# Down products' last tiles block by block, x split block by block, and table loads taken out

## The reference: two blocks of two layers each, one after the other

```
x = x + gate * (w_out(mixer(modulate(rms_norm(x)))))
u, g = split(conv3(modulate(rms_norm(x)) @ ffn_up))       # per token neighbourhood
x = x + gate' * ((silu(u) * g) @ ffn_down)                # "down": 2816 -> 1024
```

## Time and profile before

| | |
|---|---|
| median of 3 runs | 1775.49 us |
| profiled execution | 1770.85 us |
| its span | 1769.6 us |
| PE matmuls busy | 1638.8 us, 93% of the span |
| DVE / ACT / POOL busy | 963.8 / 647.9 / 467.9 us |
| granted TensorE clock, mean | 0.976 |

### The profile page before, as it was taken

One profiled execution on the slowest core, in us unless ns is written; L12 is line 12 of the kernel. 1 busy time (PEld: TensorE's weight loads), 2 busy tenths in 40 slices (PEclk: granted clock), 3 DMA queues, 4 the chain that ended last, 5 costly groups with the idle time before them and its releaser, 6 DMA issues.

```text
span 1769.6 us, 24218 instructions
## 1 busy us (share of the span) xinstructions
PE 1638.8 (93%) x9336; PEld 1314.4 (74%) x9336; DVE 963.8 (54%) x1906; ACT 647.9 (37%) x1229; POOL 467.9 (26%) x384
## 2 busy tenths in 40 slices
PE   7999999889999989989899899879999999999888
PEld 5555555358888878846567899878899998878777
DVE  4488888542222277557664788554555444233821
ACT  2442333043333332233333555443444444134511
POOL 1012201015555500022320111015555555013401
PEclk9999999999999999999999999999999999999999
DMA  9334323313222255424432455443444344325131
GB/s 350 113 119 143 103 101 120 131 71 107 96 95 96 95 169 196 159 65 156 148 126 96 155 185 182 155 148 120 132 140 145 134 133 130 125 85 182 60 125 36
DMA packets 63825, 231.16 MB, mean 131 GB/s; under 512 B 7408, under 2 KB 8432, under 8 KB 63456
## 3 DMA queue, kind: packets, MB, share of 16 engines
q1 hardware_dynamic: 60800, 218.65, 36.8%
q0 software_dynamic: 2192, 6.29, 1.1%
q10 hardware_dynamic: 720, 4.68, 0.7%
HBM read 228.55 MB, written 1.05 MB: 130 GB/s over the span
## 4 chain that ended last, share of the span: by engine, by line
PE 84%; DVE 9%; ACT 3%; issue 2%; DMA 1%; POOL 1%; SPq 0%; DVEq 0%; ACTq 0%; POOLq 0%
PE ps L232 17%; PE ps L250 10%; PE ps L251 10%; PE ps L252 10%; PE ps L1193 4%; PE ps L1194 4%; PE ps L1195 4%; PE ps L1623 3%; PE ps L724 3%; PE ps L240 3%; PE ps L714 2%; PE ps L617 2%; PE ps L294 1%; PE ps L1440 1%; PE ps L379 1%
## 5 line engine op out<-in xcount | busy, mean ns | idle before, releaser
L259 ACT ACTIVATE weights_rounded<-ring 128x1024 fp32r<-128x1024 f32 x196 | 205.0, 1053 | 108.2 <-PE ps L1195 108.2
L250 PE MATMUL ps<-h_hi,weights_rounded 128*128 128x512 f32 (+1 forms) x656 | 222.0, 338 | 5.0 <-POOL weights_rest L271 2.9
L251 PE MATMUL ps<-h_lo,weights_rounded 128*128 128x512 f32 (+1 forms) x656 | 221.6, 338 | 0.0
L252 PE MATMUL ps<-h_hi,weights_rest 128*128 128x512 f32 (+1 forms) x656 | 221.5, 338 | 0.0
L265 DVE TENSOR_TENSOR weights_rest<-ring,weights_rounded 128x1024 fp32r<-128x1024 f32 x128 | 175.3, 1371 | 76.2 <-ACT weights_rounded L259 76.1
L271 POOL TENSOR_TENSOR weights_rest<-ring,weights_rounded 128x1024 fp32r<-128x1024 f32 x68 | 163.4, 2405 | 162.7 <-ACT weights_rounded L259 162.7
L232 PE MATMUL ps<-h,ring 128*128 128x512 f32 (+1 forms) x496 | 197.9, 556 | 7.1 <-DVE h L470 7.1
L232 PEld LDWEIGHTS ps<-h,ring 128*128 128x128 f32 x496 | 95.6, 195 | 100.6 <-issue 92.6
L1164 DVE SCALAR_TENSOR_TENSOR scratch<-ps,vectors,scratch 128x510 f32<-128x510 f32 (+1 forms) x88 | 54.1, 615 | 194.6 <-ACT scratch L1124 194.4
L250 PEld LDWEIGHTS ps<-h_hi,weights_rounded 128*128 128x128 f32 x656 | 125.6, 191 | 18.7 <-POOL weights_rest L271 3.3
L1124 ACT ACTIVATE scratch<-ps,vectors 128x512 f32<-128x512 f32 (+1 forms) x88 | 59.1, 672 | 209.6 <-PE ps L252 199.1
(11 more groups left out here) (281 smaller groups left out, 3400.6 us busy)
## 6 DMA issues: line engine op xcount, KB each, us to landing
ring<-in_up SPq DMA_DIRECT2D x88, 512.0 KB, 3.5
ring<-in_ada_rest SPq DMA_DIRECT2D x80, 512.0 KB, 3.5
ring<-in_a_in SPq DMA_DIRECT2D x80, 512.0 KB, 3.5
ring<-in_down SPq DMA_DIRECT2D x44, 512.0 KB, 3.5
ring<-in_even SPq DMA_DIRECT2D x20, 512.0 KB, 3.7
ring<-in_ada_first SPq DMA_DIRECT2D x16, 512.0 KB, 8.7
ring<-in_wout SPq DMA_DIRECT2D x16, 512.0 KB, 3.5
ring<-in_odd SPq DMA_DIRECT2D x16, 512.0 KB, 4.8
```

What stands on the lines that cost most here:

```text
L250: te.matmul(bank[:, 0:n], wh[:, k, :], hi(k), start=k == 0, stop=False)
L251: te.matmul(bank[:, 0:n], wh[:, k, :], lo(k), start=False, stop=False)
L252: ins = te.matmul(bank[:, 0:n], wl[:, k, :], hi(k), start=False, stop=k == KD - 1)
L259: sc.activation(pair[0], place(*key), ACT.Copy).then_inc(*mark("rounded", *key))
```

## The change

1. `act_rsqrt` loads its table only in its first call, `(0, 0)`.
2. Down, both layers: tiles 0 to 18 as before. For tiles 19, 20 and 21 the block e becomes the outer loop: PE waits for 19 and 20, issues both for e = 0, 1, 2, waits for 21, and then goes e by e. Each bank signals when it is complete, and DVE's residual of block e waits for that bank alone. In layer 0 the mean's matmul of block e-3 is issued behind block e, and the last three at the end.
3. Layer 1: ACT rounds a0, a1, a2 within the down loop, behind the hidden blocks of j = 18, 19, 20; POOL forms their rests as soon as they are rounded, no longer behind the last residual. a1 and a2 lie in other places (`PAIR_A[4]` and `PAIR_FIRST`, in scratch), a0 and `PAIR_A[4]` move by 128 columns.
4. x is split block by block: ACT rounds block k behind residual k, DVE forms x_lo of block k-2 behind residual k. ACT's table load follows the last block.
5. Mixer a, first head: the first three products go through x together, block by block, into banks 0, 1, 2 (`pe_first_a`). Products 3, 4 and 5 follow as before, with two rotary turns behind 3 and 4 each. DVE waits for the mask behind the rotary work instead of ahead of it.

```diff
 def act_rsqrt(m, n):
-        sc.preload_act_table_set("natural_log_exp_and_others")
+        if m == (0, 0):
+            sc.preload_act_table_set("natural_log_exp_and_others")
...
 def pe_down(layer):
+        for j in range(FB - 3):
+            ready(j)
+            for e in range(KD):
+                block(j, e)
+        for j in (FB - 3, FB - 2):
+            ready(j)
+        for e in range(3):
+            block(FB - 3, e)
+            block(FB - 2, e)
+        ready(FB - 1)
+        for e in range(KD):
+            if e >= 3:
+                block(FB - 3, e)
+                block(FB - 2, e)
+            block(FB - 1, e)
+            if layer == 0 and e >= 3:
+                pe_down_mean(e - 3)
...
 def act_down(layer):
+            if layer and FB - 4 <= j < FB - 1:
+                act_round(("a", 0, j - FB + 4), a_pair(0, j - FB + 4)[0:1], a_free(0, j - FB + 4))
...
+        else:
+            for k in range(KD):
+                sc.wait_ge(*at("residual", "down", 1, k))
+                sc.activation(xhi(k), xk(k), ACT.Copy).then_inc(*mark("x_rounded", 0, k))
...
 def dve_down(layer):
-        ve.wait_ge(*at("product", "down", layer, FB - 1))
         for e in range(KD):
+            ve.wait_ge(*at("product", *down_bank(layer, e)))
...
+            if layer and e >= 2:
+                x_rest(e - 2)
...
+    def a_pair(i, s):
+        if i == 0 and s in (1, 2):
+            return (PAIR_A[4], PAIR_FIRST)[s - 1]
+        return PAIR_A[s % 5]
...
+        if i == 0 and s < 5:
+            return [[at("hidden", 1, FB - 1)], [], [at("hidden", 1, FB - 1)], [at("product", "down", 1, FB - 2)],
+                    [at("product", "a", 0, 1)]][s]
...
+    def pe_first_a():
+        for n in range(A_FIRST):
+            te.wait_ge(*at("rest_pool", "a", 0, n))
+        for k in range(KD):
+            te.wait_ge(*at("x_rest", 0, k))
+            for n in range(A_FIRST):
...
+                te.matmul(bank, wh, xhi(k), start=k == 0, stop=False)
+                te.matmul(bank, wh, xlo(k), start=False, stop=False)
+                ins = te.matmul(bank, wl, xhi(k), start=False, stop=k == KD - 1)
...
 def pe_mixer_a(i):
+            for x in ((2 * n - 6, 2 * n - 5) if i == 0 and n < 5 else (n - 1,) if n else ()):
...
 def act_mixer_a(i):
         if i == 0:
-            sc.wait_ge(*at("residual", "down", 1, KD - 1))
             sc.preload_act_table_set("exp_and_others")
-            round_tile(0, 0)
-            act_split_x(0, lambda k: at("residual", "down", 1, k))
-            round_tile(0, 1)
-            round_tile(0, 2)
...
 def pool_mixer_a(i):
         if i == 0:
+            for s in range(A_FIRST):
+                rest(0, s)
             po.wait_ge(*at("residual", "down", 1, KD - 1))
             po.dma_start(MASKA, d["masks"][:, MK_A:MK_A + 1152]).then_inc(*mark("mask_in", 2, step=16))
-            for s in range(3):
-                rest(0, s)
```

More of the change, by code:

```diff
@@ L1180, in pool_up, with down_bank, block, ready @@
                                  YS[4 * (fb % 2) + 2][:, 0:n], ALU.mult).then_inc(*mark("hidden", layer, fb))
+    def down_bank(layer, e):
+        return ("down", layer, FB - 1) if e == KD - 1 else ("down_bank", layer, e)
     def pe_down(layer):
         n = TOK if layer == 0 else SEQ
-        for j in range(FB):
+        def block(j, e):
             wh, wl = (v3(x, 128) for x in pair(j % PAIRS))
             hi, lo = (x[:, 0:n] for x in HID_T[j % 4])
-            if j == 0:
-                te.wait_ge(*at("convolved", layer, 2 * FB - 1))
+            b = BANK[e][:, 0:n]
+            te.matmul(b, wh[:, e, :], hi, start=j == 0, stop=False)
+            te.matmul(b, wh[:, e, :], lo, start=False, stop=False)
+            ins = te.matmul(b, wl[:, e, :], hi, start=False, stop=j == FB - 1)
+            if e == KD - 1:
+                ins.then_inc(*mark("product", "down", layer, j))
+            elif j == FB - 1:
+                ins.then_inc(*mark("product", *down_bank(layer, e)))
+        def ready(j):
@@ L1189, in pe_down @@
             te.wait_ge(*at("rest", "down", layer, j))
             te.wait_ge(*at("hidden_rest", layer, j))
+        te.wait_ge(*at("convolved", layer, 2 * FB - 1))
+        for j in range(FB - 3):
+            ready(j)
             for e in range(KD):
[L1192 to L1195, removed]
@@ L1196, in pe_down @@
-            ins.then_inc(*mark("product", "down", layer, j))
-        if layer == 0:
[L1198 to L1201, removed]
+                block(j, e)
[4 more added lines that the diff above has]
+            block(FB - 2, e)
@@ new lines, in pe_down, with pe_down_mean @@
+        ready(FB - 1)
[6 more added lines that the diff above has]
+                pe_down_mean(e - 3)
+        if layer == 0:
+            for e in range(KD - 3, KD):
+                pe_down_mean(e)
+    def pe_down_mean(e):
+        te.wait_ge(*at("x_squared", "down", e))
+        ins = te.matmul(BANK[0][:, 0:TOK], mean_d, sq_d[e % 2][:, 0:TOK], start=e == 0, stop=e == KD - 1)
+        ins.then_inc(*(mark("mean_part", e) if e < KD - 1 else mark("mean", (1, 0))))
@@ L1233, in dve_down, with x_rest @@
             dve_ada_bias(38, FB)
-        ve.wait_ge(*at("product", "down", layer, FB - 1))
+        def x_rest(k):
+            ve.wait_ge(*at("x_rounded", 0, k))
+            ve.tensor_tensor(xlo(k), xk(k), xhi(k).bitcast(F32), ALU.subtract).then_inc(*mark("x_rest", 0, k))
         for e in range(KD):
+            ve.wait_ge(*at("product", *down_bank(layer, e)))
             for s in ((0, 1) if layer == 0 else (1,)):
@@ L1241, in dve_down @@
             ins.then_inc(*mark("residual", "down", layer, e))
+            if layer and e >= 2:
+                x_rest(e - 2)
+        if layer:
+            x_rest(KD - 2)
+            x_rest(KD - 1)
     K1, V1 = BIG[:, 0:512], BIG[:, 512:1024]
@@ L1395, in build @@
     PTA = [BIG[:, 3456 + 512 * j:3968 + 512 * j] for j in range(4)]
-    PAIR_A = [(rounded("a_rounded_0", "big", 5504, D), rounded("a_rest_0", "big", 6528, D)), pair(0), pair(1), pair(2),
-              (rounded("a_rounded_4", "big", 7552, D), rounded("a_rest_4", "big", 8576, D))]
+    PAIR_A = [(rounded("a_rounded_0", "big", 5632, D), rounded("a_rest_0", "big", 6656, D)), pair(0), pair(1), pair(2),
+              (rounded("a_rounded_4", "big", 7680, D), rounded("a_rest_4", "big", 8704, D))]
+    PAIR_FIRST = (rounded("a_rounded_first", "scratch", 1024, D), rounded("a_rest_first", "scratch", 2048, D))
+    A_FIRST = 3
     TBA = [7, 6, 2, 5]
@@ L1446, in a_rope, with a_bank @@
         return ("a", i, x), BANK[4 + (x + 1) % 2]
+    def a_bank(i, n):
+        return BANK[n if i == 0 and n < A_FIRST else 6 + n % 2]
+    def pe_first_a():
[4 more added lines that the diff above has]
+            for n in range(A_FIRST):
+                wh, wl = (v3(w, 128)[:, k, :] for w in a_pair(0, n))
+                bank = a_bank(0, n)[:, 0:SEQ]
+                if k == 0:
+                    te.wait_ge(*at("residual", "down", 1, n))
+                te.matmul(bank, wh, xhi(k), start=k == 0, stop=False)
+                te.matmul(bank, wh, xlo(k), start=False, stop=False)
+                ins = te.matmul(bank, wl, xhi(k), start=False, stop=k == KD - 1)
+                if k == KD - 1:
+                    ins.then_inc(*mark("product", "a", 0, n))
     def pe_mixer_a(i):
@@ L1450, in pe_mixer_a @@
         if i == 0:
-            te.wait_ge(*at("x_rest", 0, KD - 2))
-        for n in range(2 * NG):
+            pe_first_a()
+        for n in range(A_FIRST if i == 0 else 0, 2 * NG):
             if n >= 2:
@@ L1456, in pe_mixer_a @@
                 te.wait_ge(*at("z_copied", "a", i - 1))
[L1457 to L1462, removed]
+            pe_product3(("a", i, n), a_pair(i, n), BANK[6 + n % 2], SEQ, xhi, xlo, "rest_pool" if n in A_POOL else "rest")
+            for x in ((2 * n - 6, 2 * n - 5) if i == 0 and n < 5 else (n - 1,) if n else ()):
+                key, work = a_rope(i, x)
+                if x >= 2:
+                    te.wait_ge(*at("rope_sin", "a", i, x - 2))
+                pe_rope(key, at("copied", *key), QA[x], ROPE2, work)
         def last_rope():
@@ L1475, in pe_mixer_a @@
         pe_product3(("a", i, 9), PAIR_A[4], BANK[6], SEQ, xhi, xlo, "rest_pool")
[L1477 to L1486, removed]
     def act_copy_out(key, bank, dst):
@@ L1536, in dve_mixer_a @@
         us, A = units_a(i), ("a", i)
[L1537 to L1539 removed]
         for n in range(2 * NG):
[L1541 removed]
+            dve_rest(("a", i, n + 3), a_pair(i, n + 3), a_free(i, n + 3))
             if n:
@@ L1546, in dve_mixer_a @@
         dve_rope(key, ROPE2, work, TA[0], [at("roped", "a", i, 3)])
+        if i == 0:
+            ve.wait_ge(*at("mask_in", 2))
         dve_maxima(us, HD ** -0.5)
```

8 lines of the change are left out of this document (3 added, 5 removed).

## The result

| | before | after |
|---|---|---|
| median | 1775.67 us (4 runs) | 1763.80 us (4 runs, 1761.65 to 1764.75) |
| ratio | | 0.9931, 95% interval 0.9916 to 0.9945 |
| profiled execution | 1770.85 us | 1762.85 us |
| its span | 1769.6 us | 1761.6 us |

The medians differ by 11.9 us, the profiled executions by 8.0, so the trace must be read by sections. I cut both spans at three instructions that both kernels have, and at one distance: the table load at the start of each down stage, the logarithm behind the first FFN, and the last gap of about 1 us on PE before the mixer's second head.

What follows compares the result with a forecast made beforehand. PE holds 84% of the chain of waits, so only its standstills or lower clock can be won. Terms -15.4 + 4.4 + 1.1 - 2.4 - 0.2 = -12.5 take the median from 1775.49 to 1763.0 us, range 1757.0 to 1768.0.

Steps and rivals of the forecast that it cites:

- A: Second FFN's last down matmul to the mixer's values: gap filled, no wait for x, 36.16 to 20.7 us, -15.4.
- the copies' wait: Mixer's first head: after three products ending together, the next waits 1.35 us for the copy of product 1.
- B: Second down tail: POOL's moved rests delay DVE, PE stops for tile 20, +4.4 us, then lower clock, +1.1.
- lower clock: Behind the stop in the second down tail: matmuls at half clock, +1.1 us, between 0 and 1.6.
- C: Behind the first FFN: mean matmuls move between products, 9.4 to 7.0 us, -2.4 (ends -1.5 and -2.8).
- D: Three of four table loads in act_rsqrt go, mostly hidden by the mean: -0.2 us, between 0 and -0.5.
- rival 4: Gap filled but time given back in the mixer's first head, under 3.5 us remain: 1773 us; chance 0.05.
- rival 3: Lower clock holds over the down tail and the mixer's first six tiles, slower than before: 1781.3 us; chance 0.03.
- no second stall: Second down tail: tile 21 follows at 1179.9 with 2.16 us of products ahead, so PE doesn't stop again.
- Rival 1: Second down tail: POOL's rests fit DVE's free 1.3 us and PE isn't stalled: 1757.5 us; chance 0.17.
- rival 2: Second down tail: POOL's rests get ahead of each DVE step, PE stalls 7 us: 1766.9 us; chance 0.17.

Runs made afterwards that it cites:

- e4: Changed kernel with the first FFN back in the old order (tile by tile, one signal, means after the last product); 1766.80 us, 0.9950 of before.
- e8: Changed kernel with the table load back in each call of act_rsqrt; 1762.86 us, 0.9922 of before.
- e1: Changed kernel, but POOL starts the rests of a0, a1, a2 only after hid_rest of tile 21; 1759.72 us, 0.9907 of before.
- e3: Changed kernel, but a0, a1, a2 are loaded, rounded and their rests formed behind down tiles 10, 13, 16; 1759.44 us, 0.9905 of before.
- e5: Changed kernel, but DVE instead of POOL forms the rests of a0, a1, a2, behind hid_rest of tile 21; 1760.75 us, 0.9908 of before.
- e2: Changed kernel, but in the second FFN only tiles 20 and 21 go block by block, tile 19 alone; 1757.51 us, 0.9891 of before.
- e6: e3, but products 3 and 4 of the mixer's first head don't wait for copies of products 1 and 2; 1756.75 us, 0.9891 of before.

## Why the prediction was right, step by step

| step | predicted | measured | by |
|---|---|---|---|
| A, gap and x split, with the copies' wait | -15.4 | -14.7 | 36.16 to 21.42 |
| B, stop for tile 20 | +4.4 | +3.95 | after, e4, e8; e1, e3, e5 take it away |
| B, lower clock | +1.1 | +2.4; in e8 +1.5 | the 72 matmuls of tiles 19 to 21 behind the stop: 10.94 us (e8 10.07), before 8.52 |
| C, behind the first FFN | -2.4 | -2.0 to -2.1 | sections before and of e4, against 133.99 |
| D, loads | -0.2 | -0.3 | e8 |
| sum | -12.5 | -10.8; -11.9 | sections; medians |

**A.** The mechanism came as played through: no wait for x, products on end. This is read from the trace; no run undoes the new x split or the block order of the first products by itself. The 0.7 us that are missing lie in the first head. The copies' wait is 1.28 (1.35 forecast). But the first matmul of the values starts 0.82 behind the one before it, of which the profile puts 0.4 to a wait for the rest of tile 8. DVE's rests meet POOL's work on the turns there: three rests are recorded with 1.59, 1.42 and 1.40 us instead of 1.22, POOL's instructions beside them with 1.59 to 1.72 instead of 0.73, and DVE stands idle for 0.63 ahead of a turn until POOL is done. POOL ends the last turn late enough for the scores to wait 0.2. That it comes of issuing the turns in pairs is likely and not tested. Of rival 4 this much happened. What I had put at nothing is that POOL's cos and add, beside DVE's rests, no longer keep within the cover of a tile.

**B.** The stop, its place, the instruction that ends it, and the order in which DVE and POOL alternate are the forecast ones; POOL's first rest is recorded 0.4 us earlier than I had it and ends 0.2 earlier. Shown by the runs: without POOL's work beside them (e1, e5) or with it in tiles that have slack (e3), the stop is gone; with an order that wants the tile later (e2), the same collision costs 0.72 and 0.33. That ACT's roundings were the cause is excluded by e1 and e5, which leave them where they are (e3 moves them too). The lower clock was mis-sized: I took 3.4 us of it, less what the stop hides, at 1.1; after the change and in e4 it held for 6.8 us, from inside the stop on, and 5.3 us of work fell into it: 2.4 (24 matmuls start in 5.26 us, which take 2.88 at the pitch of 0.12). In e8 it held for 3.4, all of it over work: 1.5. So 0 to 1.6 holds e8 and not the other two. From the row behind the long gap I had read a length as if it were a ceiling, and the same trace of before has a longer one, behind the 5.0 us stop at the head of the second down stage (PE alone):

```profile
1116.49:1122.67 6.18, 6.18 (x29) 0.50 0.74 246
```

This also takes the ground from what I set against rival 3, that the rows show only 3.4 us after each gap. One sentence was right by luck: "no second stall" ahead of tile 21 holds only because tile 20 was later still. With tile 20 in time, the order by itself stops PE there for some 0.65 us (e1, e3, e5, e6).

**C.** The loop went: 9.33 us from the first residual to the logarithm in e4 against 3.66 plus the four means ahead of it, 3.44, in the changed kernel (9.4 and 3.6 + 3.4 forecast). The products between the means got slower by 0.2 us in all, which I had left out: the last 72 products took 19.72 us with four means among them, and 16.09 without.

**D.** The size came. The 2.8 us more that I set beside it, and the 1767 in e8, misapply the sentence of the Trainium skill named under e8: it speaks of switches, and the loads taken out are none.

**Rival 1** (no collision) would have been e3's or e5's result; rival 2 needed POOL to win more often than every other time, and it never did. Rival 3 did not come, the grant came back after 6.8 us (3.4 in e8).

The terms as measured add up to 10.7, 1.8 less than forecast: nearly all of it is the lower clock and the first head, which went the same way. The sections give 10.8, with the 0.6 in them that is not the change, and without the table load of layer 1. The medians moved 11.9, 0.6 less than forecast; their interval runs from 9.8 to 14.9, so that they lie closer to the forecast than the terms do is scatter of whole runs, and luck.

## What to carry to other kernels

Before work is moved into a stage, look in the trace for engines that hold up the one that carries the new work or are held up by it, and for how much slack the consumer's order leaves: here a 0.42 us instruction became 2.6 beside GpSimd. Such collisions cost PE nothing in tiles with 2.8 us of slack (e3), and 5.5 to 6.4 us with the lower clock in a tail whose new order had none. Joining the last k tiles by output block moves each tile's due time forward; join as few as cover the work behind (here two, in the second FFN, did better than three), and check when the buffer of the last one comes free. Put rests or loads for the next stage into the middle of the present one, not at its end.

## What the runs showed of the hardware

- DVE's tensor_tensor with both inputs in SBUF and POOL's did not work at the same time in the collisions looked at, for weight rests, hid_rest and x_lo. Records overlap, but the ends don't: whichever came second ended its own length behind the other (a weight rest of DVE 1.08 us behind POOL's, POOL's 2.27 behind DVE's, hid_rest 0.28). With both queues full they took turns, one instruction each. DVE's instructions with one input in PSUM (L301, 0.42 us beside POOL's 0.73) did not slow down.
- A stop of 3.95 us on PE, behind full work, was followed by 5.3 us of work at 1.2 GHz in two traces (the changed kernel, e4), and by 3.41 in a third (e8), where it began 1.0 us behind the stop. The stops of 0.33 to 1.28 us in the down tail and the first head were followed by none.
- The same 2574 matmuls up to the first down stage took from 625.54 to 630.87 us in ten traces. The stretch of PE alone, in the kernel before and in e3:

```profile
0.00:625.54 625.54, 587.48 (x2574) 0.98 0.35 123
```

```profile
0.00:630.87 630.87, 593.77 (x2574) 0.96 0.35 122
```

  PE's busy time is 6.3 us longer at the lower mean granted clock, more than the 5.3 of the span. PE has many short stops in that stage, and how much of the work behind them falls to 1.2 GHz differs from one execution to the next. So whole runs of this kernel can't settle a microsecond. Sections between two instructions that both kernels have do better, but they hold such spells too, 1.6 us between the changed kernel and e8: a difference of that size counts only where the granted clock of both sections has been compared.
